# Forget-gate products moved sixteen slots later and cut from 24 to 16, first two decay levels moved two and one slots later

## The chip, the cores and the metric

The kernel runs on one core of a Trainium2 chip (trn2). The metric is the device time of one launch in microseconds; it ran three times, and the median counts. The engines are PE (TensorE: matrix products; its weight loads have an own row, PEld), DVE (VectorE), ACT (ScalarE), POOL (GpSimd) and SP (SyncE, which issues most DMAs).

## What is computed

Two transformer blocks in a row, on 512 tokens of width 1024, all in float32. The change lies in the second block, in the input projection and its first mixer:

```python
h = rms_norm_2(x, norm_mix_g); z = h @ w_in            # 1024 -> 6664 columns
# forgetting attention: 8 columns of z are the forget gates, one per head
logf = jax.nn.log_sigmoid(f_logit + f_bias)            # (512, 8)
c = jnp.cumsum(logf, axis=1)                           # added to the scores as c[t] - c[s]
# hgrn2 mixer, 4 heads of 128, chunks of 64 tokens
fg = lb + (1 - lb) * sigmoid(f_logit_hg); k = 1 - fg; b = cumsum(log(fg)) in the chunk
scores[t, s] = sum_c q[t, c] * k[s, c] * exp(b[t, c] - b[s, c])   for s <= t
```

The kernel takes the chunk's scores by halves: for blocks of 2m tokens (m = 32, 16, 8, 4, 2, 1) the scores between the later and the earlier half come from q * exp(b - b_mid) and k * exp(b_mid - b), and a last level gives the diagonal. These are the seven levels `hg_mm 0` to `hg_mm 6`.

## The kernel before

All large products are `w^T h` or `h^T w` in float32 made of rounded parts: each operand is split into `hi` (rounded to fp32r) and `lo` (the rest, rounded), and three products `lo*hi + hi*lo + hi*hi` are added in PSUM. The weights come by DMA in slots of 128 x 512 (`w_raw`, four of them); ACT writes `w_hi` (line 862), POOL writes `w_lo = w_raw - w_hi` (line 661), into a ring of eight slots. A slot gives PE 12 products (four tiles of 128 columns, three products each), line 1650. SP loads a raw slot when ACT and POOL are done with the slot four before it.

The order of the work is written out by hand. `make_schedule()` gives one list of steps, and every engine runs through the same list in order, doing its part of each step. A phase (`hf`, `hq`, `hi`, `hg`, `fq`, `fk`, `fv`, then gates and branches) has eight slots here. `run(names, plan)` puts behind slot number n of the stretch: the `fill` of the slot eight further on (ACT's `hi`, POOL's `lo`; ACT's part waits until PE has used the slot whose place it takes), at the end of a phase the `take` of its four PSUM tiles (banks 0 to 3; DVE or ACT; the next phase's tile n waits for it), and then the steps that `plan` names for n. Slots 0 to 7 of the stretch are `hi`, 8 to 15 `hg`, 16 to 23 `fq`, 24 to 31 `fk`. Where "slot n" is said below, this number is meant.

The steps that matter:

- `foxf 0` (PE, lines 1785 to 1791): 8 x 3 products of the normalised tokens with the eight gate columns `wf_hi`, `wf_lo` into 8 rows of bank 5. `foxf 1` (DVE 1507 to 1523, ACT 1023 to 1027): bias, log-sigmoid and cumulative sum of the 8 x 512 gates in `fx`. `foxf 2` (ACT 1028): DMA of the result to DRAM, from where the attention reads it much later.
- `hg_prep x` (DVE 1306 and 1307: the two halves of the differences of b into `hE`; ACT 1046: exponential). It waits until the key and query products of level x-1 are done.
- `hg_qk x` (DVE 1318: `hQ = hq * hE`; POOL 723: `hK = hk * hE`). It waits for the exponential and until PE is done with the level before.
- `hg_mm x` (PE 1805): 64 or 128 small products for the four heads, into banks 4 to 7, one bank for each head (head 1 has bank 5). It waits for `hQ` and `hK` of its level and for each bank.
- `hg_merge x` (DVE 1329): four masked copies from these banks into `hS`, each of which frees its bank.
- `take hi` (slot 7: ACT 981 takes tiles 0 and 2, DVE 1126 tiles 1 and 3), `take hg` (slot 15: DVE 1121).
- Then `hg_scale` (slots 20 to 23; DVE 1335, 1338, 1343), `hg_kt` (slot 25, PE 1813).

At a level's slot the plan has, in this order: `hg_mm x`, `hg_prep x+1`, `hg_merge x`, `hg_qk x+1`. `hg_prep 0` and `hg_qk 0` stand at the last slot of `hq`, just ahead of slot 0. `bank_uses()` walks through the list and counts for each step which use of its bank it is; `bank_wait` waits for all earlier ones.

Of the kernel before, what the change touches and what calls it, by code (L numbers as in the profile page):

```python
# [16 lines left out]
F32 = mybir.dt.float32  # L17
# [6 lines left out]
P = 128  # L24
# [90 lines left out]
def make_schedule():  # L115
    s = []

    def run(names, plan=(), fill=True):


        behind = {}
        for at, step in plan:
            behind.setdefault(at, []).append(step)
        n = 0
        for name in names:
            name, _, only = name.partition(":")
            p = PH[name]
            for g in range(p.groups) if not only else [int(only)]:
                for k in range(p.kc):
                    s.append(("slot", name, g, k))  # L130
                    if fill and k < p.kc - by_tile(name, g):
                        s.append(("fill", name, g, k))
                    if by_tile(name, g) == 2 and k == p.kc - 2:

                        behind[n + 1] = behind.pop(n, []) + behind.get(n + 1, [])
                    elif k == p.kc - 1 and (by_tile(name, g) < 4 or name == "pgate"):

                        s.append(("take", name, g, 0, 4))
                        if fill:
                            s.extend(("fill", name, g, kk) for kk in range(p.kc - min(by_tile(name, g), 2), p.kc))  # L140
                    s.extend(behind.pop(n, ()))
                    n += 1
        assert not behind, behind

    def attention(kind, first, last):

        room = [min(i, STEPS - 1) % TB + 5 for i in range(STEPS + LAG + 1)]
        return [(first + sum(room[:i]) * (last - first + 1) // sum(room), ("att", kind, i))
                for i in range(len(room))]

    def head_norms(q, k, first, first_k, every_k):

        tiles = [(at + every * n // 2, x, n) for x, at, every in ((q, first, 3), (k, first_k, every_k)) for n in range(4)]
        return sorted([(at + 2, ("scale", x, n)) for at, x, n in tiles]
                      + [(at, ("square", x, n)) for at, x, n in tiles], key=lambda x: x[0])

    def residual(name, norm, plan=()):


        tile = ("unscaled", "x_square", "x_add")  # L160
        run([name + ":0"])
        run([name + ":1"], [(1 + j // 2, (what, norm, j)) for j in range(4) for what in tile] + list(plan))
        for n in range(4):
            s.extend([("take", name, 1, n, n + 1), ("unscaled", norm, 4 + n), ("x_square", norm, 4 + n)])
            if n:
                s.append(("x_add", norm, 3 + n))
        s.append(("x_add", norm, 7))
        s.extend(("fill", name, 1, k) for k in range(PH[name].kc - by_tile(name, 1), PH[name].kc))

    s.append(("start",))  # L170
    run(["qA", "kA", "vA", "qB", "kB", "vB", "gateA", "branchA", "gateB"],
        [(5, ("sumsq", 0)), (5, ("rstd", 0)), (9, ("rtok", 0)), (8, ("vec", 1)), (13, ("masks",))]
        + head_norms("qA", "kA", 9, 17, 3) + attention("A", 26, 52) + attention("B", 53, 85)
        + [(at, ("curve", "gateA", g)) for g, at in enumerate((56, 64))] + [(80, ("curve", "gateB", 0))])
    run(["branchB"], [(0, ("curve", "gateB", 1))])
    residual("out1", 1)
    s.append(("up", "up1"))
    residual("down1", 2, [(4, ("foxw",))])
    levels = []
    for x, at in enumerate((2, 5, 9, 12, 15, 19, 22)):  # L180
        levels.append((at, ("hg_mm", x)))
        if x < 5:
            levels.append((at, ("hg_prep", x + 1)))
        levels.append((at, ("hg_merge", x)))
        if x < 5:
            levels.append((at, ("hg_qk", x + 1)))
    run(["hf", "hq"], [(1, ("sum", 2)), (4, ("sumsq", 2)), (4, ("rstd", 2)), (7, ("rtok", 2)), (7, ("curve", "hf", 0)),
                       (15, ("curve", "hq", 0)), (7, ("hg_decay",)), (15, ("hg_prep", 0)), (15, ("hg_qk", 0))])
    run(["hi", "hg", "fq", "fk", "fv", "gateH", "branchH", "gateF"],
        [(0, ("foxf", 0)), (1, ("foxf", 1)), (5, ("foxf", 2))] + levels  # L190
        + [(20 + i, ("hg_scale", i)) for i in range(4)] + [(25, ("hg_kt",))]
        + [(26 + 2 * q, ("hg_state", q)) for q in range(TB)]
        + [(35 + 2 * p, ("hg_out", p)) for p in range(TB + 1)]
        + head_norms("fq", "fk", 25, 34, 4) + [(44, ("foxc",)), (24, ("curve", "hg", 0))]
        + attention("F", 48, 79) + [(56, ("curve", "gateH", g)) for g in range(2)])
    run(["branchF"], [(0, ("curve", "gateF", g)) for g in range(2)])
    residual("out2", 3)
    s.append(("up", "up2"))
    residual("down2", 4, [(4, ("pT",))])
    run(["pproj", "pgate"], [(1, ("sum", 4)), (4, ("sumsq", 4)), (4, ("rstd", 4)), (6, ("rtok", 4))] + [(at, ("xback", j)) for j, at in enumerate((5, 6, 7, 8, 8, 9, 9, 10))])  # L200
    return s
# [118 lines left out]
def two_block_kernel(nc, a, out):  # L320
    ctx = ExitStack()
    with ctx:
# [37 lines left out]
        xstat = place("xstat", [P, TB])  # L360
        hstat = place("hstat", [P, TB, 3, HH])
        wf_raw = place("wf_raw", [P, DC, NH])
        wf_hi = place("wf_hi", [P, DC, NH], F32R)
        wf_lo = place("wf_lo", [P, DC, NH], F32R)
        cT = fx[:, 0, :]
        rstd = place("rstd", [P, S])
        rtok = place("rtok", [P, 3, TB])
# [1018 lines left out]
        def _(e):  # L1386
# [27 lines left out]
            for x in SCHEDULE:  # L1414
# [87 lines left out]
                elif what == "up":  # L1502
                    up_dve(e, x[1], sum_rest)
                elif what == "foxw":
                    e.wait_ge(ff["w_hi"], 1)
                    e.tensor_tensor(wf_lo[:, :, :], wf_raw[:, :, :], wf_hi[:, :, :].bitcast(F32), ALU.subtract).then_inc(ff["w_lo"], 1)
                elif x == ("foxf", 1):

                    e.wait_ge(ff["mm"], 1)
                    e.wait_ge(small_full, 32)  # L1510
                    b, use = USE[("foxf", 0)]
                    e.wait_ge(rstd_ready, 3)
                    link(e.tensor_tensor(fx[:, 0, :], ps[b][0:NH, :], rstd[0:NH, :], ALU.mult))
                    e.nop().then_inc(bank_free[b], 1)
                    link(e.tensor_scalar(fx[:, 0, :], fx[:, 0, :], fbias[:, 0:1], None, ALU.add))
                    e.scalar_tensor_tensor(out=fx[:, 1, :], in0=fx[:, 0, :], scalar=-1.0, in1=fx[:, 0, :],
                                           op0=ALU.mult, op1=ALU.min).then_inc(ff["x"], 1)
                    e.wait_ge(ff["l"], 1)
                    link(e.scalar_tensor_tensor(out=fx[:, 1, :], in0=fx[:, 0, :], scalar=0.0, in1=fx[:, 1, :],
                                                op0=ALU.min, op1=ALU.subtract))  # L1520

                    link(e.tensor_tensor_scan(fx[:, 2, :], fx[:, 1, :], fx[:, 1, :], 0.0, ALU.add, ALU.bypass))
                    e.tensor_scalar(cT, fx[:, 2, :], -1.0, None, ALU.mult).then_inc(ff["c"], 1)
                elif what in ("hg_decay", "hg_prep", "hg_qk", "hg_merge", "hg_scale", "hg_state", "hg_out"):
                    hg_dve(e, x, link)
                elif what == "pT":
                    for c in range(2):
                        b, use = USE[("pT", c)]
                        e.wait_ge(p_hi, c + 1)
                        link(e.tensor_tensor(pT_lo[:, c, :], ps[b][:, :], pT_hi[:, c, :].bitcast(F32), ALU.subtract))  # L1530
                        e.nop().then_inc(bank_free[b], 1)
                    e.nop().then_inc(p_lo, 1)
                elif what == "xback":
                    j = x[1]
                    b, use = USE[x]
                    e.wait_ge(xback_done, j + 1)
                    link(e.tensor_copy(xback[:, j, :], ps[b][:, :]))
                    e.nop().then_inc(bank_free[b], 1)
                    e.nop().then_inc(xback_ready, 1)
# [51 lines left out]
        def _(e):  # L1591
# [104 lines left out]
            for x in SCHEDULE:  # L1696
# [88 lines left out]
                elif x == ("foxf", 0):  # L1785
                    bank = bank_wait(e, x)
                    e.wait_ge(ff["w_lo"], 1)
                    for k in range(DC):
                        for i, (l, r) in enumerate(((wf_lo, h_hi), (wf_hi, h_lo), (wf_hi, h_hi))):
                            mm = e.matmul(bank[0:NH, :], l[:, k, :], r[:, k, :], start=k == 0 and i == 0, stop=k == DC - 1 and i == 2)  # L1790
                    mm.then_inc(ff["mm"], 1)
                elif what == "hg_mm":
                    lev = x[1]
# [98 lines left out]
```

## Time and profile before

| | us |
|---|---|
| median of three runs (lowest to highest) | 1579.41 (1578.83 to 1580.74) |
| profiled execution, whole | 1579.64 |
| its span, first to last instruction | 1577.9 |
| PE busy in the span | 1565.9 (99%) |
| DVE / ACT / POOL busy | 642.9 / 693.4 / 754.7 |
| mean granted TensorE clock, share of full | 0.999 |

Times in the rows are microseconds from the start of the span. A product's duration (0.39 us) overlaps with the next one's, since products are pipelined: what a product costs is the distance between the starts of two of them. A wait of PE is seen as a gap between two starts.

### The profile page before, as it was taken

The numbers are of one execution on the slowest core, as the hardware profiler recorded it, in microseconds if no ns is written. First come the engines' busy times: TensorE is split into PE (matmuls) and PEld (weight loads), VectorE is DVE, ScalarE is ACT, GpSimd is POOL, SyncE is SP. The second block draws the span as 40 slices with busy tenths as digits, with TensorE's granted clock in tenths as the row PEclk, the third lists the DMA queues.
The fourth block names the chain that finished last, engine by engine and source line by source line (L and its number), as shares of the span: only waits on it lengthen the run. The fifth ranks groups of instructions, "written<-read, shape, count | busy, mean of one in ns | idle before, by whom it ended". The sixth has DMA issues, their size and how long they took to land.

```text
span 1577.9 us, 23446 instructions
## 1 busy us (share of the span) xinstructions
PE 1565.9 (99%) x8030; PEld 1256.7 (80%) x8030; DVE 642.9 (41%) x1075; ACT 693.4 (44%) x1196; POOL 754.7 (48%) x585
## 2 busy tenths in 40 slices
PE   8999999999999999999999999999999999999999
PEld 7876777788888888888877887768888888888887
DVE  5334356444355444220477543543342122210234
ACT  5555455433544444332543644655453333322342
POOL 6632365644644554444578434323544444444441
PEclk9999999999999999999999999999999999999999
DMA  5422222223323333333232323222333333332331
GB/s 184 143 80 61 74 74 60 75 81 87 112 83 99 106 100 93 100 100 88 80 88 76 93 69 132 69 67 74 101 94 100 100 93 100 107 100 94 97 96 61
DMA packets 103352, 145.60 MB, mean 92 GB/s; under 512 B 11109, under 2 KB 57166, under 8 KB 103134
## 3 DMA queue, kind: packets, MB, share of 16 engines
q1 hardware_dynamic: 103102, 142.30, 30.3%
q10 hardware_dynamic: 160, 2.11, 0.3%
q8 instruction: 55, 0.90, 0.2%
q14 instruction: 35, 0.29, 0.1%
HBM read 142.24 MB, written 2.13 MB: 91 GB/s over the span
## 4 chain that ended last, share of the span: by engine, by line
PE 95%; DVE 2%; ACT 1%; issue 1%; POOL 1%; DMA 1%; SPq 0%; DVEq 0%; ACTq 0%; POOLq 0%
PE bank L1650 86%; PE bank L1560 2%; PE bank L1587 2%; PE bank L1575 2%; POOL w_lo L661 1%; DMA xtok<-in_x 0%; PE bank L1805 0%; PE bank L1636 0%; ACT L869 0%; PE bank L1828 0%; PE bank L1845 0%; ACT hE L1046 0%; PE bank L1781 0%; PE bank L1839 0%; PE bank L1866 0%
## 5 line engine op out<-in xcount | busy, mean ns | idle before, releaser
L661 POOL TENSOR_TENSOR w_lo<-w_raw,w_hi 128x512 fp32r<-128x512 f32 x516 | 695.7, 1357 | 782.2 <-ACT w_hi L862 781.5
L862 ACT ACTIVATE w_hi<-w_raw 128x512 fp32r<-128x512 f32 x516 | 319.0, 628 | 651.1 <-PE bank L1650 579.1
L1650 PE MATMUL bank<-h_hi,w_lo 128*128 128x512 f32 x1244 | 490.0, 394 | 0.8 <-ACT hv L981 0.7
L1650 PE MATMUL bank<-h_hi,w_hi 128*128 128x512 f32 x1244 | 484.6, 390 | 0.0
L1650 PE MATMUL bank<-h_lo,w_hi 128*128 128x512 f32 x1244 | 484.1, 389 | 0.0
L1650 PEld LDWEIGHTS bank<-h_hi,w_lo 128*128 128x128 f32 x1244 | 233.5, 188 | 51.1 <-issue 2.3
L1650 PEld LDWEIGHTS bank<-h_hi,w_hi 128*128 128x128 f32 x1244 | 233.5, 188 | 49.3
L1650 PEld LDWEIGHTS bank<-h_lo,w_hi 128*128 128x128 f32 x1244 | 233.7, 188 | 46.9
L1245 DVE TENSOR_TENSOR bank<-bank,rstd 128x512 f32<-128x512 f32 x88 | 60.1, 700 | 261.6 <-PE bank L1650 261.6
L1650 PE MATMUL bank<-g_hi,w_lo 128*128 128x512 f32 x352 | 137.0, 389 | 0.0
L1650 PE MATMUL bank<-g_hi,w_hi 128*128 128x512 f32 x352 | 136.9, 389 | 0.0
L1650 PE MATMUL bank<-g_lo,w_hi 128*128 128x512 f32 x352 | 136.9, 389 | 0.0
L1144 DVE TENSOR_TENSOR xT<-bank,xT 128x512 f32<-128x512 f32 x32 | 22.0, 688 | 206.5 <-PE bank L1650 204.5
L1650 PEld LDWEIGHTS bank<-g_hi,w_hi 128*128 128x128 f32 x352 | 66.1, 188 | 13.8
L1650 PEld LDWEIGHTS bank<-g_hi,w_lo 128*128 128x128 f32 x352 | 66.1, 188 | 13.7
L1650 PEld LDWEIGHTS bank<-g_lo,w_hi 128*128 128x128 f32 x352 | 66.1, 188 | 13.6
L1650 PE MATMUL bank<-w_lo,h_hi 128*128 128x512 f32 x184 | 73.6, 400 | 0.4 <-DVE fk L1118 0.4
L1650 PE MATMUL bank<-w_hi,h_hi 128*128 128x512 f32 x184 | 71.9, 391 | 0.0
L1650 PE MATMUL bank<-w_hi,h_lo 128*128 128x512 f32 x184 | 71.7, 390 | 0.0
L1254 DVE SCALAR_TENSOR_TENSOR acc<-bank,vec,acc 128x511 f32<-128x511 f32 x88 | 62.9, 746 | 13.2 <-ACT acc L817 8.1
L779 ACT ACTIVATE work<-work,mneg 128x128 f32<-128x128 f32 (+3 forms) x64 | 36.0, 562 | 32.7 <-DVEq L1228 17.1
L1650 PE MATMUL bank<-mix_hi,w_hi 128*128 128x512 f32 x128 | 49.8, 389 | 0.0
(297 smaller groups left out, 1781.0 us busy)
## 6 DMA issues: line engine op xcount, KB each, us to landing
w_raw<-in_w_in SPq DMA_DIRECT2D x168, 256.0 KB
w_raw<-in_w_ffn_up SPq DMA_DIRECT2D x88, 256.0 KB
w_raw<-in_w_ffn_down SPq DMA_DIRECT2D x88, 256.0 KB
w_raw<-in_w_ffn_gate SPq DMA_DIRECT2D x88, 128.0 KB
w_raw<-in_w_ffn_up SPq DMA_DIRECT2D x88, 128.0 KB
w_raw<-in_w_out SPq DMA_DIRECT2D x32, 256.0 KB
w_raw<-in_w_branch_a SPq DMA_DIRECT2D x16, 256.0 KB
w_raw<-in_w_branch_b SPq DMA_DIRECT2D x16, 256.0 KB
```

Of the source, the lines that this page charges most:

```text
L661: e.tensor_tensor(w_lo[:, pos % SPLIT_SLOTS, :], w_raw[:, pos % RAW_SLOTS, :], w_hi[:, pos % SPLIT_SLOTS, :].bitcast(F32), ALU.subtract).t ...
L779: e.activation(ring, ring, ACT.Exp, scale=-1.0, bias=mneg[:, k, j:j + 1], accum_out=rsum[:, k, j:j + 1]).then_inc(a_["e_ready"], 1)
L862: e.activation(w_hi[:, pos % SPLIT_SLOTS, :], w_raw[:, r, :], ACT.Copy).then_inc(hi_full, 1)
L1144: e.tensor_tensor(xT[:, j, :], bank, xT[:, j, :], ALU.add).then_inc(x_ready, 1)
L1245: e.tensor_tensor(ps[banks + n][:, :], ps[banks + n][:, :], rstd[:, :], ALU.mult).then_inc(q["scaled"], 1)
L1254: e.scalar_tensor_tensor(out=o, in0=ps[banks + n][:, 0:S - shift], scalar=vec[:, conv_col(tap, col, n // 2)], in1=o, op0=ALU.mult, op1=ALU ...
L1560: e.matmul(banks[h][:, 0:n], qk1[qn][r, pair, qb * P:n], qk1[kn][r, pair, 0:n], start=True, stop=True).then_inc(a_["sc_done"], 1)
L1575: mm = e.matmul(bank[64 * h:64 * h + 64, c * P:S], vtok[vn][:, c, d], probs_t[kind][:, h, c, c * P:S], start=c == 0, stop=c == TB - 1, ski ...
L1587: mm = e.transpose(bank[:, o:o + P], work[(2 * j + h) % 4][:, c * P:(c + 1) * P], ident[:, :])
L1650: mm = e.matmul(ps[banks + n][:, :], l, r, start=k == 0 and i == 0, stop=k == p.kc - 1 and i == 2)
```

## The change

Three edits.

1. `levels`: level 0 goes from slot 2 to slot 4, level 1 from slot 5 to slot 6. The others stay at 9, 12, 15, 19, 22.
2. `foxf 0, 1, 2` go from slots 0, 1, 5 to slots 16, 17, 18. Level 4's burst and merge (slot 15) are now ahead of `foxf 0` in the list, so that its use of bank 5 comes behind theirs.
3. `wf_hi` and `wf_lo` become columns 0 to 7 and 32 to 39 of one tile `wf` with 40 columns, zeros between. One product with all 40 columns and `h_hi` gives `hi*hi` in rows 0 to 7 and `lo*hi` in rows 32 to 39 of the bank; a second one adds `hi*lo` to rows 0 to 7. That makes 16 products for the eight parts of the depth. DVE scales both groups of rows (one multiply more) and adds them in the instruction that adds the bias. A memset of the zeros is added in `foxw`.

```diff
--- before.py
+++ after.py
@@ -177,7 +177,7 @@
     s.append(("up", "up1"))
     residual("down1", 2, [(4, ("foxw",))])
     levels = []
-    for x, at in enumerate((2, 5, 9, 12, 15, 19, 22)):
+    for x, at in enumerate((4, 6, 9, 12, 15, 19, 22)):
         levels.append((at, ("hg_mm", x)))
         if x < 5:
             levels.append((at, ("hg_prep", x + 1)))
@@ -187,7 +187,7 @@
     run(["hf", "hq"], [(1, ("sum", 2)), (4, ("sumsq", 2)), (4, ("rstd", 2)), (7, ("rtok", 2)), (7, ("curve", "hf", 0)),
                        (15, ("curve", "hq", 0)), (7, ("hg_decay",)), (15, ("hg_prep", 0)), (15, ("hg_qk", 0))])
     run(["hi", "hg", "fq", "fk", "fv", "gateH", "branchH", "gateF"],
-        [(0, ("foxf", 0)), (1, ("foxf", 1)), (5, ("foxf", 2))] + levels
+        levels + [(16, ("foxf", 0)), (17, ("foxf", 1)), (18, ("foxf", 2))]
         + [(20 + i, ("hg_scale", i)) for i in range(4)] + [(25, ("hg_kt",))]
         + [(26 + 2 * q, ("hg_state", q)) for q in range(TB)]
         + [(35 + 2 * p, ("hg_out", p)) for p in range(TB + 1)]
@@ -360,8 +360,9 @@
         xstat = place("xstat", [P, TB])
         hstat = place("hstat", [P, TB, 3, HH])
         wf_raw = place("wf_raw", [P, DC, NH])
-        wf_hi = place("wf_hi", [P, DC, NH], F32R)
-        wf_lo = place("wf_lo", [P, DC, NH], F32R)
+
+        wf = place("wf", [P, DC, 32 + NH], F32R)
+        wf_hi, wf_lo = wf[:, :, 0:NH], wf[:, :, 32:32 + NH]
         cT = fx[:, 0, :]
         rstd = place("rstd", [P, S])
         rtok = place("rtok", [P, 3, TB])
@@ -1502,6 +1503,7 @@
                 elif what == "up":
                     up_dve(e, x[1], sum_rest)
                 elif what == "foxw":
+                    link(e.memset(wf[:, :, NH:32].bitcast(F32), 0.0))
                     e.wait_ge(ff["w_hi"], 1)
                     e.tensor_tensor(wf_lo[:, :, :], wf_raw[:, :, :], wf_hi[:, :, :].bitcast(F32), ALU.subtract).then_inc(ff["w_lo"], 1)
                 elif x == ("foxf", 1):
@@ -1511,8 +1513,10 @@
                     b, use = USE[("foxf", 0)]
                     e.wait_ge(rstd_ready, 3)
                     link(e.tensor_tensor(fx[:, 0, :], ps[b][0:NH, :], rstd[0:NH, :], ALU.mult))
+                    link(e.tensor_tensor(fx[:, 1, :], ps[b][32:32 + NH, :], rstd[32:32 + NH, :], ALU.mult))
                     e.nop().then_inc(bank_free[b], 1)
-                    link(e.tensor_scalar(fx[:, 0, :], fx[:, 0, :], fbias[:, 0:1], None, ALU.add))
+                    link(e.scalar_tensor_tensor(out=fx[:, 0, :], in0=fx[:, 0, :], scalar=fbias[:, 0:1], in1=fx[:, 1, :],
+                                                op0=ALU.add, op1=ALU.add))
                     e.scalar_tensor_tensor(out=fx[:, 1, :], in0=fx[:, 0, :], scalar=-1.0, in1=fx[:, 0, :],
                                            op0=ALU.mult, op1=ALU.min).then_inc(ff["x"], 1)
                     e.wait_ge(ff["l"], 1)
@@ -1786,8 +1790,8 @@
                     bank = bank_wait(e, x)
                     e.wait_ge(ff["w_lo"], 1)
                     for k in range(DC):
-                        for i, (l, r) in enumerate(((wf_lo, h_hi), (wf_hi, h_lo), (wf_hi, h_hi))):
-                            mm = e.matmul(bank[0:NH, :], l[:, k, :], r[:, k, :], start=k == 0 and i == 0, stop=k == DC - 1 and i == 2)
+                        e.matmul(bank[0:32 + NH, :], wf[:, k, :], h_hi[:, k, :], start=k == 0, stop=False, skip_group_check=True)
+                        mm = e.matmul(bank[0:NH, :], wf_hi[:, k, :], h_lo[:, k, :], start=False, stop=k == DC - 1, skip_group_check=True)
                     mm.then_inc(ff["mm"], 1)
                 elif what == "hg_mm":
                     lev = x[1]
```

## Rows read from the trace of the kernel before

**Rows 1.** The page: span, PE's busy time, the chain that ended last by line
```profile
span 1577.9 us, 23446 instructions
...
PE 1565.9 (99%) x8030; PEld 1256.7 (80%) x8030; DVE 642.9 (41%) x1075; ACT 693.4 (44%) x1196; POOL 754.7 (48%) x585
...
PE bank L1650 86%; PE bank L1560 2%; PE bank L1587 2%; PE bank L1575 2%; POOL w_lo L661 1%; DMA xtok<-in_x 0%; PE bank L1805 0%; PE bank L1636 0%; ACT L869 0%; PE bank L1828 0%; PE bank L1845 0%; ACT hE L1046 0%; PE bank L1781 0%; PE bank L1839 0%; PE bank L1866 0%
```

**Rows 2.** Waits of PE, the longest: line, waited for, us in total, times, longest
```profile
PE bank L1805 <- issue: 2.4, 1, 2.4
```

**Rows 3.** Timeline of PE: start, length, line, operation [idle before <- releaser]
```profile
799.49 0.40 PE L1790 MATMUL bank<-h_hi,wf_lo 128*8 128x512 f32 x1
...
805.02 0.39 PE L1650 MATMUL bank<-w_lo,h_hi 128*128 128x512 f32 x1
...
810.55 1.21 PE L1805 MATMUL bank<-hQ,hK 128*32 128x32 f32 x64
...
822.55 1.31 PE L1805 MATMUL bank<-hQ,hK 128*32 128x16 f32 x128 [2.40 <-issue]
...
830.24 0.47 PE L1650 MATMUL bank<-h_hi,w_lo 128*128 128x512 f32 x1 [0.71 <-ACT hv L981]
...
831.01 0.47 PE L1650 MATMUL bank<-h_hi,w_lo 128*128 128x512 f32 x1
...
859.36 0.39 PE L1650 MATMUL bank<-h_hi,w_lo 128*128 128x512 f32 x1
...
877.25 1.35 PE L1805 MATMUL bank<-hq,hk 128*32 128x32 f32 x128
...
886.83 1.91 PE L1813 MATMUL bank<-ident,hK 128*128 128x128 f32 x16
```

**Rows 4.** Timeline of DVE, gates and `hg_prep`, 805 to 828 us
```profile
805.64 0.67 DVE L1513 TENSOR_TENSOR fx<-bank,rstd 8x512 f32<-8x512 f32 x1
...
814.27 0.41 DVE L1523 TENSOR_SCALAR fx<-fx 8x512 f32<-8x512 f32 x1
814.62 1.21 DVE L1306 TENSOR_TENSOR hE<-hb 128x1024 f32<-128x1024 f32 x1
...
822.48 2.28 DVE L1306 TENSOR_TENSOR hE<-hb 128x1024 f32<-128x1024 f32 x1 [2.25 <-POOL hK L723]
```

**Rows 5.** POOL: timeline, then line 661 (shortest, median, longest in ns)
```profile
804.61 3.37 POOL L723 TENSOR_TENSOR hK<-hk,hE 128x1024 f32<-128x1024 f32 x1 [3.99 <-ACT hE L1046]
...
819.10 3.35 POOL L723 TENSOR_TENSOR hK<-hk,hE 128x1024 f32<-128x1024 f32 x1 [5.94 <-issue]
...
L661 POOL TENSOR_TENSOR w_lo<-w_raw,w_hi x8: 1277/1603/2277, 807.9 to 833.7; 128x512 fp32r<-128x512 f32 x8
```

**Rows 6.** Weight loads of 32 columns: shortest, median, longest in ns
```profile
L1805 PEld LDWEIGHTS bank<-hQ,hK x704: 106/109/113, 810.6 to 868.7; 128*32 128x32 f32 x176
```

**Rows 7.** A raw load in the chain; timeline of ACT around the take
```profile
794.69 2.67 DMA w_raw<-in_w_in
...
828.91 0.61 ACT L862 ACTIVATE w_hi<-w_raw 128x512 fp32r<-128x512 f32 x1
829.43 1.25 ACT L981 ACTIVATE hv<-bank,rtok 128x512 f32<-128x512 f32 x2
```

**Rows 8.** DVE and POOL from level 4 on; line 1306's six halves
```profile
856.13 2.21 POOL L661 TENSOR_TENSOR w_lo<-w_raw,w_hi 128x512 fp32r<-128x512 f32 x1 [0.30 <-ACT w_hi L862]
...
859.63 1.34 DVE L1329 COPY_PREDICATED hS<-level_mask,bank 128x256 f32<-128x256 uint32 x2 [0.21 <-DVE hE L1307]
...
861.96 3.55 DVE L1318 TENSOR_TENSOR hQ<-hq,hE 128x1024 f32<-128x1024 f32 x1
868.13 2.51 DVE L1329 COPY_PREDICATED hS<-level_mask,bank 128x256 f32<-128x256 uint32 x4 [2.62 <-PE bank L1805]
...
882.78 3.01 DVE L1343 TENSOR_TENSOR hK<-hK,hk 128x2048 f32<-128x2048 f32 x1
...
L1306 DVE TENSOR_TENSOR hE<-hb x6: 1206/1758/2300, 798.2 to 856.0; 128x1024 f32<-128x1024 f32 x6
```

## The prediction

> **What bounds the kernel now.** The page comes first: TensorE (PE) is busy 99% of the span and the chain that ended last runs through its products, 86% of it on line 1650 alone [rows 1]. So work taken from PE pays in full, and work on VectorE (DVE), ScalarE (ACT) or GpSimd (POOL) counts only where PE waits. The list of PE's waits is led by 2.4 us ahead of a `hg_mm` burst (line 1805) [rows 2]. The PE timeline places it, and a second one: level 1's burst starts at 822.55 after 2.40 us of nothing, and `hg` tile 0 at 830.24 after 0.71 us for ACT's take of `hi` [rows 3]. Behind that, tile 1 starts at 831.01 and not three products (0.68) after 830.24, another 0.1 us. The 24 products of slots 1 and 2 fill 805.02 to 810.55: 0.227 us each and a tenth at the edge of the burst, so 2.72 for a slot of twelve. The gates' 24 keep nearly that pace, 799.49 to 805.02, 0.230 each [rows 3].
>
> What holds level 1 is not PE. DVE ran the gates' `fx` steps from 805.64 to 814.68, and `hg_prep 1` (lines 1306, 1307) stood behind them until 814.62 [rows 4]. From there 7.8 us pass over exponential and key product (line 723) until 822.45, when POOL is done and PE may start [rows 4, 5].
>
> **The change part by part.** I work each step on the clock of the profiled run and look where PE stands at two marks: `hg` tile 1 (831.01) and the first product of a slot behind the moved gates.
>
> 1. The gates' products leave slot 0: 24 x 0.230 = 5.5 us less on PE [rows 3]. They return in slot 16 as 16 x 0.230 = 3.7 us. The wider weights (40 columns) cost nothing: a load of 32 takes 0.109 us at the median [rows 6], and if time went with columns one of 40 would take 0.136 (an estimate from that row), under the 0.227 between products. The net is -1.8 us, if nothing else moved.
> A rule of the pages would give less: the Trainium skill, "TensorE: Matmul & The Clock Gate", section "Back-to-back issue gap", has about 131 ns for each sustained product of 512 columns. By it eight products would be 1.0 us and not 1.8; the rows say 227 to 230 ns, and I use them.
>
> 2. Level 0 moves from slot 2 to slot 4. PE gets there at 799.49 + 4 x 2.72 + 0.1 = 810.5, as before (810.55); its keys are ready at 807.98 [rows 3, 5]. No wait.
>
> 3. Level 1. PE would reach it, behind burst 0 (1.2) and slots 5 and 6, at 810.5 + 1.2 + 2 x 2.72 + 0.1 = 817.2 [rows 3]. DVE is free of `fx`, so `hg_prep 1` can start at 808.1, when key product 0 is done, and not at 814.62. But there it meets POOL, which has its `w_lo` subtractions (line 661) to do, and because the plan is in order, those of slots 0 to 4 (five, where before three) come ahead of key product 1. Now the rows on DVE and POOL together: a half of `hg_prep` takes 1.21 us while POOL is idle and 2.28 while it subtracts; a subtraction takes 1.28 alone and up to 2.27 beside it [rows 4, 5]. So they take turns and a turn costs the other some 1.1 us. Counted as one queue from 807.93: five subtractions 5 x 1.28 = 6.4, three turns of DVE (two halves, the query product of line 1318, which also reads two tiles) 3.3, and the key product without the turn in it 3.35 - 1.1 = 2.2. The key product ends at 819.8, 2.7 us before 822.45. The fifth subtraction is not held by its load: the raw slot is free when the first subtraction is done (809.2), the load takes 2.67 [rows 7], ACT's copy 0.6, which makes 812.5, and it is due in the queue only at 815. PE waits 2.6 us at level 1, as long as before.
> The rule behind it stands in the Trainium skill, "SBUF — State Buffer", section "Who interferes with whom": DVE instructions with two SBUF inputs and GpSimd instructions that read SBUF lock each other out. By it the three turns are whole; the trace agrees (2.28 against 1.21). Without it the third rival's time would hold.
>
> 4. The take of `hi` (slot 7). ACT takes tile 0 only behind the exponential of `hg_prep 2`, and DVE takes tile 1 only behind the query product, both tied to the end of key product 1. From it to `hg` tile 1 were 831.01 - 822.45 = 8.56 us [rows 3, 5]. Now only slot 7 lies between burst 1 and this point, and slots 6 and 7 did before, so PE arrives earlier and waits longer: 819.9 + 1.2 + 2.8 = 823.9, against 819.8 + 8.5 = 828.3. ACT's `w_hi` copy of 0.5 us that stood between exponential and take [rows 7] now comes first, but DVE's take of tile 1 isn't helped by that, and I count nothing. So at this mark PE is 831.01 - 828.3 = 2.7 us ahead: of the 5.5 us taken off, 2.8 became waiting.
>
> 5. Levels 2 to 4 keep their slots and their distances to this mark; their waits were zero and stay so. All shifts by -2.7: burst 4 at 852.6.
>
> 6. The gates in slot 16. PE is at their first product at 859.36 - 2.7 = 856.7. They want bank 5, which since the move is filled by level 4 (head 1) and freed by DVE's merge. In this trace the merges of heads 0 and 1 run from 859.63 to 860.97 [rows 8], behind the take of `hg` and `hg_prep 5`, which hang on PE's slot 15 and shift with it: free at 858.3. PE waits 861.0 - 859.3 = 1.7 us in order, with slot 17 and all behind it queued. In the old place the bank had long been free. Then 3.7 us of products: all behind is later by -2.7 + 1.7 + 3.7 = +2.7 us. Below nothing this wait can't be; its upper end is given with the slower rival.
>
> 7. `fx` in slot 17. DVE is free of query product 5 at 865.5 - 2.7 = 862.8 (ends of rows 8), the products are done at 862.1. The chain took 814.68 - 805.64 = 9.0 us [rows 4]; the second multiply adds 0.7; it ends at 872.5. Behind it wait merge 5 (2.5 us) and `hg_scale` 0 and 1, which I take at 2.3 each, below the 2.5 of the merge and the 3.0 of line 1343, until 879.6 [rows 8]. Merge 6 waits for PE's burst at 877.25 + 2.7 = 880.0 anyway, and the product of line 1343 ended 1.0 us before PE's transposes [rows 3, 8]. So it is hidden, with 0.9 and then 1.0 us to spare. ACT stands at the wait for `c` meanwhile (slot 18, to 872.5); its `w_hi` copies are eight slots (22 us) ahead of use. The memset and the sparser `wf_lo` are done in `down1`, where DVE waits for PE: nothing. The attention that needs the saved rows starts in slot 48: nothing.
>
> Sum: +2.7 us. The profiled execution had a span of 1577.9 and 1.74 around it, 1579.64 in all, 0.23 above the median of 1579.41. I forecast 1579.41 + 2.7 = 1582.1 us.
>
> **The rivals.**
> - *Slower by more (1583.2 to 1584.3).* `hg_prep 5`'s first half ran in 1.21 because POOL's subtraction began at 856.13, 0.15 us after it [rows 8]. If it begins first, that half loses a turn of 1.1, merge 4 is that much later and PE waits 2.8 at bank 5: +3.8. It decides from a shift of 0.15 us between DVE and POOL. A further turn ahead of key product 1 adds 1.1 again: +4.9. For it: of the six first halves, the shortest took 1.21 and the longest 2.30, with a median of 1.76 [rows 8], so half of them lost a turn. Against: both engines follow PE's slots there and should keep their order.
> - *The waits dissolve (1574.5).* The edit does what its placing would suggest: level 1 and the take of `hi` no longer wait and bank 5 is free. Then -5.5 - 2.4 - 0.7 + 3.7 = -4.9. Against: the in-order queue of POOL and the merge behind `hg_prep 5` stand in the rows.
> - *No turns between DVE and POOL (1578.3).* If key product 1 comes as soon after `hg_prep 1` as it did, 7.8 us, it ends at 815.9; then PE is not late at level 1, `hg` tile 1 is at 815.9 + 8.6 = 824.5, 6.5 ahead, and the sum is -6.5 + 1.7 + 3.7 = -1.1. For it: in this trace that stretch was as short. Against: POOL was idle then.
>
> **How the numbers follow.** Forecast case 0.58, with its own range +1.5 to +3.9 (each of three turns half as long or longer); slower rival 0.23; no turns 0.14; waits dissolve 0.05. This kernel's measurement tells about 0.2%, 3.2 us, from no change. The forecast lies just inside; about 0.12 of its 0.58 lies beyond. Slower: 0.23 + 0.12 = 0.35; same: 0.46 + 0.14 = 0.60; faster: 0.05. The range goes from the third rival's 1578.3 to 1583.8, in the middle of the slower one, and leaves out the rest of that and the dissolved waits.
>
> **What would show it.** In the changed profile: 16 gate products near 858 to 862; a wait of PE ahead of them near 1.7 us, released by the DVE merge; a wait of about 2.6 at the level 1 burst near 819.9, released by POOL; one of 3 us or more at `hg` tile 0, released by ACT. `hg_prep 1` should start at 808.1 with two halves of 2.3, key product 1 should end near 819.8. If that end is at 816, or the gates' first product starts without a wait, the prediction is wrong and the time lower; if burst 5 comes later than 870.3, it is higher.

## The result

The changed kernel takes 1581.38 us (median of 20 runs, 1580.77 to 1584.25) against 1579.58 for the kernel before (20 runs beside them). The ratio is 1.0015, with a 95% interval of 1.0008 to 1.0021: 1.3 to 3.3 us slower, 2.4 by the ratio itself (the two medians are 1.8 us apart). The forecast was +2.7, 1582.1 us.

I measure the stretch by one distance, free of what happens earlier in an execution: from the first product of `hi` (slot 0) to the first transpose of `hg_kt` (slot 25). Both are starts in the timeline of PE. Before they are 796.75 (the row below) and 886.83 [rows 3], 90.1 us apart; after 795.83 and 888.37, 92.5 apart. So the 2.4 us are in this stretch. The span grew by 1.5 only, because this execution of the changed kernel happened to reach the stretch 0.9 us earlier (796.75 - 795.83): at the very start PE waited 0.5 us for the loads of `x` in it and 1.6 in the other.

```profile
796.75 0.40 PE L1650 MATMUL bank<-w_lo,h_hi 128*128 128x512 f32 x1
```

**Profile after.** Waits of PE (line, waited for, us in total, times, longest), to be read beside [rows 2]:

```profile
PE bank L1809 <- issue: 2.3, 1, 2.3
PE bank L1654 <- ACT hv L982: 1.5, 1, 1.5
PE bank L1793 <- DVE hS L1330: 1.5, 1, 1.5
...
PE bank L1654 <- DVE hv L1127: 0.3, 1, 0.3
```

The wait at level 1 is as long as before (2.3 against 2.4). The third line is new: the gates' products (1793) wait for DVE's merge (1330). Timeline of PE, beside [rows 3]:

```profile
795.83 0.40 PE L1654 MATMUL bank<-w_lo,h_hi 128*128 128x512 f32 x1
...
818.70 1.75 PE L1809 MATMUL bank<-hQ,hK 128*32 128x16 f32 x128 [2.28 <-issue]
820.38 0.80 PE L1654 MATMUL bank<-w_lo,h_hi 128*128 128x512 f32 x1
...
821.40 0.63 PE L1654 MATMUL bank<-w_hi,h_hi 128*128 128x512 f32 x1
821.83 0.63 PE L1654 MATMUL bank<-w_lo,h_hi 128*128 128x512 f32 x1
...
825.85 0.47 PE L1654 MATMUL bank<-h_hi,w_lo 128*128 128x512 f32 x1 [1.54 <-ACT hv L982]
...
827.11 0.50 PE L1654 MATMUL bank<-h_hi,w_lo 128*128 128x512 f32 x1 [0.33 <-DVE hv L1127]
...
857.13 0.43 PE L1793 MATMUL bank<-h_hi,wf 128*40 128x512 f32 x1 [1.47 <-DVE hS L1330]
...
860.61 0.40 PE L1794 MATMUL bank<-h_lo,wf 128*8 128x512 f32 x1
860.84 0.40 PE L1654 MATMUL bank<-h_hi,w_lo 128*128 128x512 f32 x1
...
888.37 1.91 PE L1817 MATMUL bank<-ident,hK 128*128 128x128 f32 x16
```

The gates' sixteen products take 857.13 to 860.84, 3.7 us, after 1.5 us of waiting. Tile 1 of `hg` starts 31.3 us behind the first `hi` product (827.11 - 795.83); before it was 34.3. The products at 821.40 and 821.83 are 0.43 us apart, not 0.23. DVE and POOL in the same stretch, beside [rows 4, 5]:

```profile
807.10 2.30 DVE L1307 TENSOR_TENSOR hE<-hb 128x1024 f32<-128x1024 f32 x1 [2.29 <-POOL hK L724]
809.33 2.29 DVE L1308 TENSOR_TENSOR hE<-hb 128x1024 f32<-128x1024 f32 x1
...
855.77 2.50 DVE L1330 COPY_PREDICATED hS<-level_mask,bank 128x256 f32<-128x256 uint32 x4 [0.21 <-DVE hE L1308]
...
867.86 1.33 DVE L1527 TENSOR_SCALAR fx<-fx 8x512 f32<-8x512 f32 x1
869.66 2.50 DVE L1330 COPY_PREDICATED hS<-level_mask,bank 128x256 f32<-128x256 uint32 x4 [0.47 <-PE bank L1809]
...
875.98 2.29 DVE L1339 TENSOR_TENSOR hQ<-hq,hE 128x2048 f32<-128x2048 f32 x1 [1.70 <-ACT hE L1053]
```

```profile
803.70 3.37 POOL L724 TENSOR_TENSOR hK<-hk,hE 128x1024 f32<-128x1024 f32 x1 [3.98 <-ACT hE L1047]
807.02 9.25 POOL L662 TENSOR_TENSOR w_lo<-w_raw,w_hi 128x512 fp32r<-128x512 f32 x5
816.23 2.36 POOL L724 TENSOR_TENSOR hK<-hk,hE 128x1024 f32<-128x1024 f32 x1
```

`hg_prep 1` starts right behind key product 0, both halves take 2.3 us, and POOL's five subtractions fill the 9.25 us to key product 1, without a gap. Key product 1 ends at 818.59, 22.8 us behind the first `hi` product (before: 25.7). The merge of level 4, at 855.77, is what the gates wait for. The row of DVE at 867.86 is the last of the `fx` steps, which began at 861.55.

### The profile page after: what moved, and what is told of

It is laid out like the page before. It is cut to its first block, busy times and chain, and to the rows that moved or that the text cites. A ratio compares the mean times of both kernels' runs of the same rounds, so it can differ in the third digit from the quotient of the medians.

```text
span 1579.4 us, 23433 instructions
## 1 busy us (share of the span) xinstructions
PE 1566.0 (99%) x8022; PEld 1257.3 (80%) x8022; DVE 644.1 (41%) x1077; ACT 693.4 (44%) x1196; POOL 753.5 (48%) x585
## 4 chain that ended last, share of the span: by engine, by line
PE 96%; DVE 1%; POOL 1%; DMA 1%; issue 1%; ACT 0%; SPq 0%; DVEq 0%; POOLq 0%; ACTq 0%
PE bank L1654 87%; PE bank L1564 2%; PE bank L1591 2%; PE bank L1579 2%; DMA xtok<-in_x 0%; PE bank L1640 0%; ACT hE L1047 0%; POOL hK L724 0%; POOL w_lo L662 0%; PE bank L1809 0%; DVE hE L1308 0%; PE bank L1832 0%; PE bank L1849 0%; PE bank L1785 0%; PE bank L1843 0%
## 5 line engine op out<-in xcount | busy, mean ns | idle before, releaser
L1654 PE MATMUL bank<-mix_hi,w_lo 128*128 128x512 f32 x128 | 49.8, 389 | 0.0
```

Of the source, the lines that this page charges most:

```text
L1654: mm = e.matmul(ps[banks + n][:, :], l, r, start=k == 0 and i == 0, stop=k == p.kc - 1 and i == 2)
```

## The experiments

All distances are from the first `hi` product, in us, in each kernel's profiled execution; "key 1" is the end of key product 1, "tile 1" the start of tile 1 of `hg`. The ratio is to runs of the kernel before on the same chip. The intervals of the ratios are some 1.5 us wide to either side, so a difference of 1 to 2 us between two of these kernels is clear of noise only where their intervals lie apart.

| kernel | key 1 | tile 1 | `hg_mm 6` | `hg_kt` | ratio (95%) |
|---|---|---|---|---|---|
| before | 25.7 | 34.3 | 80.5 | 90.1 | |
| changed | 22.8 | 31.3 | 82.9 | 92.5 | 1.0015 (1.0008 to 1.0021) |
| 1: 16 products alone | 26.0 | 35.0 | 81.1 | 90.7 | 0.9998 (0.9989 to 1.0007) |
| 2: gates at 17 | 22.8 | 31.3 | 82.9 | 92.7 | 1.0004 (0.9995 to 1.0013) |
| 3: levels at 2, 5 | 21.3 | 30.5 | 82.0 | 91.6 | 1.0005 (0.9996 to 1.0014) |
| 4: memset for five `w_lo` | 20.5 | 29.1 | 82.3 | 91.9 | 1.0004 (0.9995 to 1.0013) |
| 5: products at 0, rest of `fx` at 17 | 21.3 | 29.9 | 76.6 | 93.2 | 1.0016 (1.0007 to 1.0025) |
| 6: as 5, levels at 4, 6 | 23.5 | 32.1 | 79.9 | 96.7 | 1.0040 (1.0027 to 1.0054) |
| 7: moves alone, 24 products | 22.8 | 31.3 | 86.4 | 95.9 | 1.0027 (1.0018 to 1.0037) |
| 8: 2 and 3 together | 21.2 | 30.5 | 80.3 | 90.1 | 0.9997 (0.9988 to 1.0006) |
| 9, 11: `fx` in gaps, 16 products | 21.3 | 30.1 | 79.0, 80.4 | 88.6, 90.0 | 0.9996, 0.9997 (0.9987 to 1.0006) |
| 10, 12: `fx` in gaps, 24 products | 21.3 | 30.8 | 77.0, 76.9 | 86.5, 86.6 | 0.9977, 0.9978 (0.9968 to 0.9987) |

**1. The cut to 16 products alone.** The changed kernel with the plan of before:

```diff
-    for x, at in enumerate((4, 6, 9, 12, 15, 19, 22)):
+    for x, at in enumerate((2, 5, 9, 12, 15, 19, 22)):
...
-        levels + [(16, ("foxf", 0)), (17, ("foxf", 1)), (18, ("foxf", 2))]
+        [(0, ("foxf", 0)), (1, ("foxf", 1)), (5, ("foxf", 2))] + levels
```

> The kernel before with only the cut from 24 to 16 products (one 40-column tile); the gates stay at slots 0, 1, 5 and the levels at 2 and 5. My theory (the chain through DVE sets level 1): PE is 1.8 us earlier at level 0, but DVE cannot start the fx steps before its query product 0 is done (805.7), and has one multiply more (0.7), so key product 1 ends 0 to 0.7 us later than before, PE's wait at level 1 grows from 2.4 to between 4.2 and 4.9, and from the first hi product to hg_kt it is 90.1 to 90.8 us (before 90.1): time as before to 0.7 us more. Rival (products pay in full, since PE is 99% busy): 88.2 us and 1.8 us less time than before.

Its rows of DVE and PE at levels 0 and 1:

```profile
806.91 0.67 DVE L1515 TENSOR_TENSOR fx<-bank,rstd 8x512 f32<-8x512 f32 x1
...
816.14 1.21 DVE L1307 TENSOR_TENSOR hE<-hb 128x1024 f32<-128x1024 f32 x1
```

```profile
809.99 1.21 PE L1809 MATMUL bank<-hQ,hK 128*32 128x32 f32 x64
824.06 1.63 PE L1809 MATMUL bank<-hQ,hK 128*32 128x16 f32 x128 [4.49 <-issue]
```

PE comes 1.8 us earlier to level 0 (12.0 behind the first product, before 13.8) and then waits 4.5 instead of 2.4. The `fx` steps last 9.3 us on DVE and set level 1, so key product 1 ends 0.3 us later; the other 0.3 us of the 0.6 at `hg_kt` go with products 0.43 us apart behind the wait (some five of them; run 2 shows what that is). Theory held: the ratio is 0.9998, and the rival's 1.8 us less lies just outside its interval, which reaches down to 1.7 us less. In front of a wait that another engine ends, eight products less are worth nothing, although PE is 99% busy.

**2. The gates one slot later.**

```diff
-        levels + [(16, ("foxf", 0)), (17, ("foxf", 1)), (18, ("foxf", 2))]
+        levels + [(17, ("foxf", 0)), (18, ("foxf", 1)), (19, ("foxf", 2))]
```

> The changed kernel with the gates one slot later (17, 18, 19). My theory: bank 5 is free by then, PE's 1.5 us wait ahead of the gates' products goes and nothing takes its place: 92.55 - 1.5 = 91.1 us from the first hi product to hg_kt, about 0.9 us more time than before. Rival (the wait is given back: DVE's fx steps, a slot later, now delay merge 5, hg_scale and hg_kt): 92.5 us, as the changed kernel, +2.4.

The ratio went from 1.0015 to 1.0004, 1.7 us, near the theory's 1.5, though the two intervals overlap, and the list of PE's waits has none for line 1793 any more. But the profiled execution reads 92.7, which is the rival's number. What filled it is none of the rival's steps: PE's products ran at twice their spacing for a while behind tile 0. Stretches of this kernel (busy us and counts of PE, PEld, DVE, ACT, POOL; then PEclk, the granted clock as a share of full speed, 2.4 GHz):

```profile
826.00:829.00 3.00, 1.88 (x7) 1.29 (x8) 2.55 (x3) 1.76 (x4) 2.79 (x1) 0.98 0.01 3
829.00:832.00 3.00, 3.00 (x9) 2.33 (x8) 2.41 (x2) 0.29 (x1) 1.80 (x2) 0.50 0.09 10
832.00:836.00 4.00, 4.00 (x141) 3.16 (x139) 1.80 (x4) 1.49 (x3) 2.19 (x2) 0.97 0.35 98
```

From 829 to 832 the granted clock was at its lower level, 1.2 GHz. The same is seen in the changed kernel, there behind level 1:

```profile
818.00:820.00 2.00, 1.30 (x111) 1.33 (x115) 1.37 (x1) 0.00 (x0) 2.00 (x3) 0.74 0.23 86
820.00:822.00 2.00, 2.00 (x37) 1.68 (x30) 2.00 (x2) 0.00 (x0) 2.00 (x1) 0.50 0.48 128
```

In the changed kernel it cost nothing: it made PE some 1.6 us late for tile 0 of `hg`, where it would have waited anyway (1.5 us of waiting instead of 3.1, an estimate of the wait at the full pace of 0.227 us). In this one it came behind that wait, and eight products at 0.43 us cost 8 x 0.20 = 1.6 us. So 92.5 - 1.5 + 1.6 = 92.6.

**3. Levels 0 and 1 back at slots 2 and 5.**

```diff
-    for x, at in enumerate((4, 6, 9, 12, 15, 19, 22)):
+    for x, at in enumerate((2, 5, 9, 12, 15, 19, 22)):
```

> The changed kernel with levels 0 and 1 back at slots 2 and 5; the gates stay at 16. My theory (POOL's in-order queue sets key product 1): only three w_lo subtractions stand ahead of it instead of five, 2.5 us less: it ends 20.4 us behind the first hi product (changed 22.8, before 25.7), hg tile 1 starts near 29.0 (changed 31.3), and hg_kt 90.2 us behind it, the time as before (+0.1). PE then waits some 3 us at level 0, which costs nothing. Rival (the later slots of the levels are what keeps PE from waiting, as their placing suggests): the 3 us at level 0 come on top, 95.5 us and +5 us against before.

POOL, beside the three rows of the changed kernel above:

```profile
805.43 3.30 POOL L724 TENSOR_TENSOR hK<-hk,hE 128x1024 f32<-128x1024 f32 x1 [4.02 <-ACT hE L1047]
808.69 5.74 POOL L662 TENSOR_TENSOR w_lo<-w_raw,w_hi 128x512 fp32r<-128x512 f32 x3
815.40 3.39 POOL L724 TENSOR_TENSOR hK<-hk,hE 128x1024 f32<-128x1024 f32 x1 [0.98 <-issue]
```

Three subtractions instead of five, and key product 1 ends 1.5 us earlier, although PE is let wait 2.9 us at level 0 for it. I had expected 2.5: with three subtractions POOL is done first and idle for 0.98 us, and the halves of `hg_prep 1` and ACT's exponential set the key product. `hg_kt` is at 91.6 and not at 90.2. Of these 1.4 us, 0.9 are this later key product, and some 0.6 the clock, which was low again behind the 2.9 us wait: run 5 has its key product at the same 21.3 and no low clock there, and its tile 1 comes at 29.9 instead of 30.5. The products at 0.43 us, which cost the changed kernel nothing, cost something here. Over all runs the ratio is 1.0005: by the ratios the later slots of the levels made the kernel slower by 1.6 us (1.1 between runs 2 and 8), not faster; the intervals overlap, and the trace is what shows the 1.5 us at key product 1. The rival's 95.5 is out.

**4. No subtraction ahead of key product 1.**

```diff
+                if isinstance(pos, int) and 268 <= pos <= 272:
+                    e.memset(w_lo[:, pos % SPLIT_SLOTS, :].bitcast(F32), 0.0).then_inc(lo_full, 1)
+                    return
                 e.tensor_tensor(w_lo[:, pos % SPLIT_SLOTS, :], w_raw[:, pos % RAW_SLOTS, :],
```

> The changed kernel, but POOL writes w_lo of the five slots hg 0 to hg 4 by a memset, which reads nothing, in place of the subtraction (their rests are left out of the result). My theory (turns between DVE and POOL and the length of POOL's queue set key product 1): hg_prep 1's halves take 1.2 us each and not 2.3, key product 1 ends 2 to 3 us earlier, near 20.2 us behind the first hi product, hg_kt at 90.0 instead of 92.55. Rival (raw loads or ACT's copies hold the queue, not POOL's own work): key product 1 stays near 22.8 and hg_kt near 92.5.

```profile
808.17 1.23 DVE L1310 TENSOR_TENSOR hE<-hb 128x1024 f32<-128x1024 f32 x1 [2.28 <-POOL hK L727]
809.31 1.22 DVE L1311 TENSOR_TENSOR hE<-hb 128x1024 f32<-128x1024 f32 x1
```

```profile
811.46 0.63 ACT L866 ACTIVATE w_hi<-w_raw 128x512 fp32r<-128x512 f32 x1 [2.75 <-DMA w_raw<-in_w_in]
...
812.15 0.52 POOL L663 MEMSET w_lo<- 128x512 f32 x1 [2.15 <-ACT w_hi L866]
```

The halves take 1.23 and 1.22 us beside POOL's memsets, and 2.30 and 2.29 beside its subtractions. Key product 1 ends at 20.5, 2.3 us earlier: DVE and POOL do take turns, and this queue was the limit. How much of the 2.3 us is the turns is not told apart, since a memset (0.52 us) is also shorter than a subtraction (1.28 alone). With POOL quick the supply of slots is the next limit: ACT waits 2.75 us for the raw load of the fifth slot, the exponential of `hg_prep 1` stands behind that copy on ACT, and POOL's fifth memset waits 2.15 us for it. The gain in the traced `hg_kt` is 0.6 only, again with the clock low behind the wait for ACT (2.9 us); by the ratio it is 1.7 us, with overlapping intervals.

**5. The products at slot 0, DVE's part split.** Levels 0 and 1 are at slots 2 and 5. DVE frees bank 5 at once with the two multiplies; bias, log-sigmoid and cumulative sum (new step `foxf 3`) stay late.

```diff
+        [(0, ("foxf", 0)), (1, ("foxf", 1)), (17, ("foxf", 3)), (18, ("foxf", 2))] + levels
...
                     e.nop().then_inc(bank_free[b], 1)
+                elif x == ("foxf", 3):
                     link(e.scalar_tensor_tensor(out=fx[:, 0, :], in0=fx[:, 0, :], scalar=fbias[:, 0:1], in1=fx[:, 1, :],
```

> 16 products as in the changed kernel, but at slot 0 as before, with levels 0 and 1 at slots 2 and 5; DVE does only the two multiplies that free bank 5 there (1.4 us) and the rest of fx (sum, log-sigmoid, cumulative sum) at slot 17, the save at 18. My theory (PE's products are free where PE would wait anyway, and level 1 hangs on DVE's fx steps and POOL's queue): no wait at level 0 and none at level 1 (burst 0 at 12.0, key product 1 at 20.5, burst 1 at 21.5 us behind the first hi product), hg tile 1 near 29.3, no wait at bank 5, hg_kt at 84.9 to 85.8 (before 90.1, changed 92.55): 4.3 to 5.2 us less time than before. With no wait of PE over 1.5 us the products should also show no spacing of 0.43 us, twice the usual, as four of the five changed kernels' traces show behind such a wait. Rival (the products and the extra multiply pay in full wherever they stand): the bank wait of 1.5 saved at most, 91 us, +1 us against before.

Waits of PE, and then the stretch behind the first of them (columns as in run 2):

```profile
PE bank L1655 <- DVE fq L1119: 4.1, 1, 4.1
...
PE bank L1655 <- ACT hv L982: 0.7, 1, 0.7
```

```profile
880.00:887.00 7.00, 5.48 (x13) 4.35 (x14) 5.36 (x6) 0.00 (x0) 0.73 (x1) 0.52 0.34 98
```

Up to `hg_mm 6` it came nearly as expected: burst 0 at 12.0, burst 1 at 21.5, no wait at the bank; key product 1 was 0.8 us later than said (21.3) and tile 1 0.6 (29.9); burst 6 at 76.6, 3.9 us ahead of before. Then DVE, which had lost 8 us to `fx` at slot 17 with no wait of PE in that place to cover it, took `fq` too late: PE stood for 4.1 us at tile 0 of `fk`, and the clock was low for most of the 7 us after it. The expectation had left out the take of `fq` (slot 23) as a due of DVE. With `hg_kt` at 93.2 and a ratio of 1.0016 neither the theory's total (4.3 to 5.2 us less) nor the rival's (1 us more, 91) held.

**6. The same with levels at 4 and 6.**

```diff
-    for x, at in enumerate((2, 5, 9, 12, 15, 19, 22)):
+    for x, at in enumerate((4, 6, 9, 12, 15, 19, 22)):
```

> As the run with the gates' first part at slot 0, but levels 0 and 1 at slots 4 and 6 as in the changed kernel. My theory (five subtractions of POOL ahead of key product 1 against three): key product 1 at 22.8 us behind the first hi product, burst 1 without a wait at 24.1, a wait of some 4 us at hg tile 0 and 1, tile 1 at 31.3, hg_kt at 87.1, or up to 1.7 later if the products behind that wait run at twice their spacing: 1.3 to 3 us less time than before, and 2 us or more behind the run with levels at 2 and 5. Rival (the levels' slots don't matter once PE has the products at slot 0): 85 us as that run.

Key 1 and tile 1 came within 0.8 us of the expectation and 2.2 behind run 5, so the levels' slots matter here too. The rest fell with the take of `fq` (4.6 us) and two low stretches of the clock, eight and ten products long: 96.7 and a ratio of 1.0040, where the theory had 87.1 to 88.8 and the rival 85.

**7. The moves alone, 24 products.** The kernel before with the new plan (the diff of run 1 the other way round).

> The kernel before with only the moves: 24 products at slot 16, levels at 4 and 6. My theory (where the products stand alone, each costs its 0.23 us): everything as in the changed kernel up to the gates, then 8 x 0.230 = 1.8 us more, less 0.0 to 0.7 hidden for the multiply that is left out: hg_kt at 94.4 us behind the first hi product (changed 92.55), time 4.2 us above before. Rival (DVE's merge and fx steps hide the products): 92.6 us, as the changed kernel.

Equal to the changed kernel up to tile 1, then the products: 5.3 us from the first to the last, against 3.5 with 16. The ratio of 1.0027 against 1.0015 is 1.9 us. The intervals of the two ratios just overlap, so it is the trace (5.3 against 3.5) that shows the price: where the gates stand in the changed kernel, the eight products are worth their 1.8 us in full. The traced 95.9 has one more stretch of products at 0.43 (eight of them, behind tile 1) than the expected 94.4.

**8. Gates at 17 and levels at 2 and 5.**

> The changed kernel with levels at 2 and 5 and the gates at 17: both single edits together. My theory: hg_kt at 91.6 - 1.5 = 90.1 us behind the first hi product if the stretch of doubled spacing behind the 3.3 us wait at level 0 comes again (88.4 to 88.7 without it): the time of before within 0.5 us, 2 us below the changed kernel. Rival (the bank wait, once gone, comes back as another wait, since moving the gates alone brought 92.7): 91.6 us or more.

90.1 as expected with the low stretch, ratio 0.9997. Its interval lies apart from that of the changed kernel, 1.0008 to 1.0021, so this difference (2.8 us by the ratios, 2.4 in the traces) is clear of noise. With both places put right, key product 1 behind five subtractions and the wait at bank 5, the whole loss of the change is gone.

**9 and 11. `fx` in the gaps of DVE, 16 products.** The edit is shown against run 5.

```diff
-        [(0, ("foxf", 0)), (1, ("foxf", 1)), (17, ("foxf", 3)), (18, ("foxf", 2))] + levels
+        [(0, ("foxf", 0)), (1, ("foxf", 1)), (3, ("foxf", 3)), (10, ("foxf", 4)), (11, ("foxf", 2))] + levels
...
+                elif x == ("foxf", 4):
                     e.wait_ge(ff["l"], 1)
                     link(e.scalar_tensor_tensor(out=fx[:, 1, :], in0=fx[:, 0, :], scalar=0.0, in1=fx[:, 1, :],
```

> 16 products at slot 0, levels 0 and 1 at slots 2 and 5, and DVE's fx steps laid into its gaps instead of at slot 17: the two multiplies that free bank 5 at slot 1, bias and minimum (with ACT's exponential and logarithm) at slot 3, difference, cumulative sum and negation at slot 10, the save at 11. My theory (the run with the rest of fx at slot 17 was 3.85 us ahead of before at burst 6 and lost that and more because DVE came 4 us late with the take of fq): nothing holds DVE now, hg tile 1 at 29.9 us behind the first hi product, burst 6 at 76.2, hg_kt at 85.8 (before 90.1): 4.3 us less time than before, 1575.3. Rival (another of DVE's dues is as tight as the take of fq, so moved steps are paid wherever they go): hg_kt later than 88.5, less than 1.5 us won.

> The same kernel as the run with 16 products and spread fx steps, once more. There PE stood for 2.5 us behind the 120th of the 128 small products of level 4, with no wait for another engine in the profile, and hg_kt came at 88.6 us instead of 85.8. If this stop belongs to the program (the place of these instructions), it comes again at the same product, hg_kt is at 88.6 and the time 1.5 us below before. If it was chance of one execution, hg_kt is at 86.0 and the median near that of the kernel with 24 products, 3.5 to 4 us below before.

```profile
850.76 1.25 PE L1811 MATMUL bank<-hQ,hK 128*32 128x16 f32 x120
854.46 0.26 PE L1811 MATMUL bank<-hQ,hK 128*32 128x16 f32 x8 [2.46 <-issue]
```

PE stops inside level 4's burst, 8 products before its end, for 2.5 us, with no engine that it waits for. In the second run it stopped behind the same product for 2.45 us; there the clock was low behind the stop, and `hg_kt` came at 90.0, not at the expected 88.6. In the first, without the stop, it would have been at 86.1. Run 5 has a stop behind the same product too, of 0.33 us. Run 1 gives PE the same products in the same order and has none, so the list of PE's work alone does not make it; that it came again shows that it belongs to this program, but its cause is not shown. Of the 4.3 us forecast for this kernel, 0.5 to 0.6 are left by the ratios, and their intervals reach beyond 1.

**10 and 12. `fx` in the gaps, 24 products.** The kernel before with the plan and the two new steps of run 9; the products, their tiles and DVE's one multiply as before.

> The same laying out of the fx steps in the kernel before, so with 24 products of 8 columns at slot 0, one multiply at slot 1, and 53 fewer lines changed: it asks what the eight products saved are worth where PE has waits behind them. My theory (key product 1 and the take behind it set hg tile 1, not PE): burst 0 at 13.8, burst 1 at 23.3, hg tile 1 between 30.0 and 30.3, so 0.1 to 0.4 us behind the run with 16 products, hg_kt near 86.1: 4 us less time than before. Rival (products pay in full): 1.8 us behind the run with 16, hg_kt at 87.6.

> The same kernel as the run with 24 products and spread fx steps, once more beside the one with 16 on one chip. My theory (the eight products are worth little where PE has waits behind them, and this version has no stop in its bursts): hg_kt at 86.5 again, time 3.5 us below before (ratio 0.9978), and so below both kernels of the study. Rival (the first measurement was lucky): ratio above 0.999.

```profile
795.17 0.39 PE L1652 MATMUL bank<-w_lo,h_hi 128*128 128x512 f32 x1
...
809.00 1.21 PE L1807 MATMUL bank<-hQ,hK 128*32 128x32 f32 x64
818.52 1.32 PE L1807 MATMUL bank<-hQ,hK 128*32 128x16 f32 x128
...
881.71 1.91 PE L1815 MATMUL bank<-ident,hK 128*128 128x128 f32 x16
```

No bracket with a wait is left on PE's rows of this stretch, and the granted clock stays up. 881.71 - 795.17 = 86.5. Both measurements agree: 1576.25 and 1575.83 us, 0.9977 and 0.9978, so 3.5 us below the kernel before and, by the ratios, 5 to 6 below the changed one. This is the version that beats both. Beside run 9 without its stop, eight products fewer would be worth 0.8 us at tile 1 (30.1 against 30.8) and 0.4 at `hg_kt`, more than the 0.1 to 0.4 I had put on tile 1, but far from 1.8.

## Why the prediction was right, step by step

1. **Products.** 0.230 us each: 16 took 3.7 us, and the 40 columns cost nothing. Run 7 has the same price by the ratio (1.9 us for eight). The 131 ns for a sustained product that the Trainium skill has in "TensorE: Matmul & The Clock Gate", section "Back-to-back issue gap", are not borne out here: the starts of these products are 227 to 232 ns apart.
2. **Level 0** had no wait: held.
3. **Level 1.** Key product 1 was forecast 23.05 us behind the first `hi` product (819.8 - 796.75) and came at 22.8; PE's wait was 2.3 where 2.6 was said. The parts: five subtractions with DVE's turns in 9.25 us (said 9.7), the key product without its turn 2.36 (said 2.2). The two halves lost a turn each, as said; the third turn was smaller, as the query product took 1.46 us and not 2.3. Run 4 shows the turns, run 3 the two subtractions. The one-queue sum has a limit that I had not written down: with three subtractions ACT's exponential is later than POOL (run 3), and it is valid only because five stand there.
4. **Take of `hi`.** Tile 1 was forecast 31.55 behind (828.3 - 796.75) and came at 31.3. The wait ahead of tile 0 was to be 3 us or more and was 1.54, with 0.33 more for tile 1. Here the picture was wrong: in place of the missing 1.5 us stand the slower burst and the products at twice their spacing, since the clock was low at 820 to 822. The sum did not change, because both end at DVE's and ACT's takes.
5. **Levels 2 to 4** kept their distances: held (burst 4 is 24.3 behind tile 1 in both).
6. **Bank 5.** 1.47 us for the DVE merge, said 1.7; the forecast's own rows, 860.97 - 859.36, give 1.6. Runs 2 and 8 have no wait there: against run 3 run 8 is 1.5 us shorter in the trace and 1.3 by the ratio, and run 2 is 1.7 below the changed kernel by the ratio.
7. **`fx` at slot 17** was hidden: merge 5 even waited 0.47 for PE, and merge 6 1.04 (0.9 was said). But the match is luck. The chain took 7.6 us (861.55 to 869.19), not 9.7, and the sum left out that `hg_scale 1` waits 1.7 for ACT, as it does in the kernel before. With a chain of 9.7 merge 6 would have been some 0.6 us late (an estimate: 1.6 later at merge 5, less the 1.04). Also, the margin was named by the wrong step. The tight due of DVE is the take of `fq`, as run 5 shows, where PE is 6 us further ahead and loses 4.1 there.

The sum -3.0 (tile 1) + 1.5 + 3.7, and 0.2 at the edges, = +2.4 stands against -2.7 + 1.7 + 3.7 = +2.7. The slower rival's extra turn did not occur (the first half of `hg_prep 5` took 1.22 again); the waits did not dissolve; and the turns were real. The ratio of 1.0015 is inside the 0.2% that the forecast called the same, and its interval just reaches beyond. The distances are those of one execution of each kernel; that the two ends agree to 0.3 us is partly luck, since low stretches of the clock moved `hg_kt` by 1.4 us and more in other traces (runs 2, 7 and 11) and happened to cost nothing in this one.

What is open: why PE stops inside the burst in runs 9 and 11, and why the clock fell in the changed kernel's trace behind 2.3 us of waiting and did not in the kernel before behind 2.4, nor in run 2 behind 2.3 at level 1.

## What to carry to other kernels

On a bound engine an instruction is worth its time only where nobody else ends the next wait; ahead of such a wait the same eight products were worth nothing (run 1), behind it 1.8 us (run 7). When a step is moved in an order written out by hand, list for its new place what it then finds full (here a PSUM bank that frees only behind another engine's queue), and for the other moved steps what now stands ahead of them in every other queue (here two more subtractions on GpSimd). The gain lay in neither, but in splitting the VectorE work: free the bank at once, put the rest into that engine's gaps.

## What the runs showed of the hardware that I had not expected

A wait of PE can cost more than itself. In nine of the twelve traces of the experiments, and in the changed kernel's, a wait of 2.3 to 5 us in this stretch was followed by products 0.43 us apart instead of 0.23, with a granted clock of 0.50 (1.2 GHz instead of 2.4). Eight such products cost 1.6 us; behind the 4.1 us wait of run 5 there were thirteen, 2.7 us. It was free where PE was due to wait again soon (the changed kernel), and it did not come in the kernel before behind 2.4 us, nor in run 2 behind 2.3 at level 1, nor in run 9 behind its stop of 2.5 us, while in run 11 it came behind the same stop, and in run 7 a second time behind only 1.3 and 0.3 us. So the length of the wait alone does not say whether it comes. The traces of runs 10 and 12, without such waits, have none in this stretch. The Trainium skill, "SBUF — State Buffer", section "Who interferes with whom", would have a VectorE instruction with two SBUF inputs run undisturbed beside a GpSimd one that only writes; run 4 (1.23 us beside memsets, 2.30 beside subtractions) agrees.
